# First attention scores ahead of the compressed values' copies, and an output slot's split behind the second head

## What is computed

```
kvc   = silu(blocks(kv) @ cmp_w1) @ cmp_w2            # compressed keys k_cmp and values v_cmp, 15 blocks
p_cmp = softmax(q @ k_cmp * scale - slope * dist)     # branch 1
p_slc = softmax(q @ k_slc * scale - slope * dist)     # branch 2, all 4 blocks of 64 are selected
p_win = softmax(q @ k_win * scale - slope * dist)     # branch 3, window 512 > 256 tokens
o     = g0 * p_cmp @ v_cmp + g1 * p_slc @ v_slc + g2 * p_win @ v_win
x     = x + o @ w_out
```

## Time and profile before

| what | value |
|---|---|
| runs | 1428.94 us median of 3 (1428.84 to 1434.26) |
| profiled execution | 1427.04 us, of it the span of the profile 1425.3 us |
| TensorE busy | 1387.1 us, 97% of the span |
| VectorE busy | 1182.6 us, 83% |
| ScalarE busy | 1020.8 us, 72% |
| chain that ended last, by engine | PE 91%, DVE 4%, issue 1%, ACT 1%, DMA 1% |
| mean granted clock of TensorE | 0.994 |
| moved from HBM | 429.40 MB, 302 GB/s over the span |

### The profile page before, as it was taken

One profiled execution on the slowest core, in us unless ns is written; L12 is line 12 of the kernel. 1 busy time (PEld: TensorE's weight loads), 2 busy tenths in 40 slices (PEclk: granted clock), 3 DMA queues, 4 the chain that ended last, 5 costly groups with the idle time before them and its releaser, 6 DMA issues.

```text
span 1425.3 us, 19022 instructions
## 1 busy us (share of the span) xinstructions
PE 1387.1 (97%) x6962; PEld 1139.1 (80%) x6962; DVE 1182.6 (83%) x1094; ACT 1020.8 (72%) x1070; POOL 41.1 (3%) x99
## 2 busy tenths in 40 slices
PE   7999999999999989999999999999999999999996
PEld 7987888888974578788888878888878888878884
DVE  6946655547768679899999999999999999999997
ACT  6546544435557757788887888887888888788884
POOL 7000000001000000000000000000000000000000
PEclk9999999999999989999999999999999999999999
DMA  8443555554630029899999999999999999999995
GB/s 325 168 172 118 207 178 182 175 205 148 237 119 1 21 113 351 322 391 421 408 398 402 397 394 406 404 409 401 392 400 395 414 412 394 388 415 384 421 421 206
DMA packets 59995, 431.68 MB, mean 303 GB/s; under 512 B 6656, under 2 KB 6656, under 8 KB 7808
## 3 DMA queue, kind: packets, MB, share of 16 engines
q1 hardware_dynamic: 59760, 429.95, 77.2%
q10 hardware_dynamic: 144, 0.52, 0.1%
HBM read 429.40 MB, written 1.05 MB: 302 GB/s over the span
## 4 chain that ended last, share of the span: by engine, by line
PE 91%; DVE 4%; issue 1%; ACT 1%; DMA 1%; DVEq 0%; POOL 0%; POOLq 0%; SPq 0%; ACTq 0%
PE bank L1509 19%; PE bank L1511 19%; PE bank L1510 19%; PE bank L1980 7%; PE bank L1981 6%; PE bank L2060 3%; PE bank L1999 3%; PE bank L2000 3%; DVE w_lo L1376 2%; PE bank L1857 2%; PE bank L1883 2%; PE bank L1951 1%; PE bank L1867 1%; PE bank L2047 1%; DMA raw<-in_moe 1%
## 5 line engine op out<-in xcount | busy, mean ns | idle before, releaser
L1376 DVE TENSOR_TENSOR w_lo<-raw,w_hi 128x2048 fp32r<-128x2048 f32 x331 | 747.0, 2287 | 38.7 <-ACT w_hi L759 36.0
L759 ACT ACTIVATE w_hi<-raw 128x2048 fp32r<-128x2048 f32 x331 | 630.2, 1919 | 127.5 <-PE bank L1511 57.8
L1509 PE MATMUL bank<-w_hi,ht_hi 128*128 128x512 f32 (+1 forms) x768 | 299.4, 390 | 0.9 <-DVE ht_lo L908 0.9
L1511 PE MATMUL bank<-w_hi,ht_lo 128*128 128x512 f32 (+1 forms) x768 | 296.3, 386 | 0.0
L1510 PE MATMUL bank<-w_lo,ht_hi 128*128 128x512 f32 (+1 forms) x768 | 295.8, 385 | 0.0
L876 DVE TENSOR_TENSOR w_lo<-raw,w_hi 128x2048 fp32r<-128x2048 f32 x73 | 166.6, 2289 | 109.9 <-ACT w_hi L444 109.7
L444 ACT ACTIVATE w_hi<-raw 128x2048 fp32r<-128x2048 f32 x74 | 141.5, 1919 | 95.0 <-PE bank L1511 92.9
L1980 PE MATMUL bank<-w_hi,ht_hi 128*128 128x512 f32 x448 | 177.4, 396 | 1.4 <-DVE w_lo L1376 1.4
L1981 PE MATMUL bank<-w_lo,ht_hi 128*128 128x512 f32 x448 | 174.7, 390 | 0.0
L1509 PEld LDWEIGHTS bank<-w_hi,ht_hi 128*128 128x128 f32 x768 | 144.4, 188 | 29.6 <-issue 1.4
L1511 PEld LDWEIGHTS bank<-w_hi,ht_lo 128*128 128x128 f32 x768 | 144.3, 188 | 29.5
(11 more groups left out here) (338 smaller groups left out, 1666.0 us busy)
## 6 DMA issues: line engine op xcount, KB each, us to landing
raw<-in_moe SPq DMA_DIRECT2D x336, 1024.0 KB, 7.6
raw<-in_wts SPq DMA_DIRECT2D x71, 1024.0 KB, 4.9
xs<-in_x SPq DMA_DIRECT2D x2, 512.0 KB, 4.1
out<-xn SPq DMA_DIRECT2D x4, 256.0 KB, 2.0
pk<-in_packed SPq DMA_DIRECT2D x1, 517.0 KB, 7.8
g1b<-in_norm_ffn ACTq DMA_DIRECT2D x1, 512.0 KB, 3.8
gfb<-in_norm_final SPq DMA_DIRECT2D x1, 512.0 KB, 8.4
```

Of the source, the lines that this page charges most:

```text
L759: a(w_hi[:, n % SPLIT, :], raw[:, n % RAW, :], ACT.Copy).then_inc(s_hi, 1)
L1376: v.tensor_tensor(w_lo[:, n % RAW, :], raw[:, n % RAW, :], w_hi[:, n % SPLIT, :].bitcast(F32), ALU.subtract).then_inc(s_lo, 1)
L1509: mm(out_, sh, mh, start=first, stop=False)
L1511: return mm(out_, sl, mh, start=False, stop=last)
```

## The change

The first scores' wait for all six copies of the compressed keys and values is taken out. The compressed scores wait for the two key copies (`s_kc >= 2`), and the transposes of turn 1, which write the bank that the values are copied from, wait for all six. The call `split_to(BO0 + 1)` moves on ACT from ahead of turn 0's exponentials into turn 1, behind turn 2's exponentials, and on DVE from ahead of turn 0's bias into turn 1, behind turn 3's bias. The work itself is the same.

```diff
@@ scalar: behind the six copies of kc and vbd
-        split_to(BO0 + 1)
@@ scalar: in the loop over n
             if n + 1 < 2 * HB:
                 head_exp(n + 1)
+            if n == 1:
+                split_to(BO0 + 1)
             if n in (2, 8):
                 cmp_exp(n // 8)
@@ tensor: behind the compression matmuls
         ins.then_inc(s_w2, 1)
-        pe.wait_ge(s_kc, 6)
@@ tensor: behind the first scores
         for n in range(3):
             head_scores(n)
+        pe.wait_ge(s_kc, 2)
         cmp_scores(0, range(HB // 2))
@@ tensor: in the loop over n
+            if n == 1:
+                pe.wait_ge(s_kc, 6)
             head_transpose(n)
```

## The result

The changed kernel took 1440.8 us (median of 20 runs, 1430.51 to 1444.06), the kernel before, run beside it, 1429.46 us (20 runs, 1426.19 to 1434.26). The ratio is 1.0074, with a 95% interval of 1.0063 to 1.0084. That is 11.3 us slower, where the prediction had 0.7 us and a range that ended at 1432.5 us. It was wrong.

A forecast was written before the change was run, and what follows sets the result against it. PE was taken to bound the kernel (91% of the last-ending chain). Wait removed -2.12, turn 3's transposes' wait +1.7, lost lead and late copy +1.1: +0.7 us, 1429.6 us; 8-in-10 range 1426.3 to 1432.5.

The forecast's parts named there:

- cover left behind it on ACT: Idle time remaining on ACT between its moved split and the copy of turn 0's transposes: 1.7 us, so the move is free.
- Parts 1 to 3: First scores: PE gains 2.12 us; ACT's split costs nothing; DVE's two splits take 4.4 us, making compressed sums 1.36 late.
- What is late next: PE waits 1.7 us ahead of turn 3's transposes, then for group 0's product, ending 0.65 to 0.7 us behind.
- Rival A: DVE's lateness dies out before reaching PE, so the whole gap is won: -2.1 us, 1426.8 us; chance 0.18.
- The rule cited beside it: Find gaps on the busiest engine and let what their semaphores depend on start or end sooner; by it, 1426.8 us.
- Rivals B and C: B: ACT and DVE set the pace behind the splits, +1.4 to +2.3, 0.14. C: first scores still held, +2.8, 0.03.
- rival D: A new 1.7 us gap on PE brings the granted clock down to 0.50 for about 2 us: +2 more; chance 0.02.

The follow-up runs named there:

- e5: The changed kernel plus 7 spare matmuls on PE ahead of turn 3's transposes, half filling the new gap: 1429.69 us, ratio 0.9996 to the kernel before.
- e3: The changed kernel plus 14 spare matmuls on PE ahead of turn 3's transposes, filling the new gap: 1429.96 us, ratio 1.0001 to the kernel before.
- e1: The kernel before with only PE's waits moved, the splits staying ahead of the heads: 1427.39 us, ratio 0.9977.
- e2: The changed kernel with the wait for all six copies back ahead of the first scores, so only the splits are moved: 1438.85 us, ratio 1.0063.
- e6: The kernel before with ACT's split moved ahead of the key and value copies, lengthening PE's old gap to 3.02 us: 1431.51 us, ratio 1.0002.
- e7: e1 plus spare matmuls while PE waits at the router, 22 ahead of the ranks and 11 behind them: 1425.94 us, ratio 0.9966 to the kernel before.
- e9: The changed kernel plus 20 spare matmuls on PE ahead of turn 6's transposes, its gap kept: 1439.14 us, ratio 1.0061 to the kernel before.

## Why the prediction was wrong, step by step

Its steps on the schedule held. With 1.70 us taken off the times of the changed kernel (0.08 off that of e5):

| step | forecast | measured |
|---|---|---|
| idle ahead of the first scores | 0 | 0 |
| DVE's first bias | 403.1 | 404.85 - 1.70 = 403.15 |
| ACT's split | 409.6 | 411.26 - 1.70 = 409.56 |
| cover left behind it on ACT | 1.7 | 1.72 (the bracket at 414.88) |
| DVE's two splits | 414.0, 4.4 long | 413.92, 4.48 |
| compressed bias | 418.4 | 418.32 |
| ACT's scaling, turns 2 and 3 | 420.0, 424.15 | 419.91, 424.04 |
| PE's wait ahead of turn 3's transposes | 1.7 | 1.66 |
| group 0's product (clock at 1.00, e5) | near 429.0 | 429.01 - 0.08 = 428.93 |
| lag of the output projection (clock at 1.00, e3 and e5) | +0.7 | +0.55 |

**Parts 1 to 3** and **What is late next** were right, in mechanism and in size; the sum was 0.15 us too high for the schedule. The two runs of the change that held the clock, 1430.51 and 1431.04 us, are 1.1 and 1.6 us above the median of before, where the forecast had 0.7. **Rival A** didn't come: the whole gap is won in e1 (2.19 us), without the second half of the change, and not in the change itself. The rule cited beside it from the Trainium skill, "Perfetto Trace Analysis", section "Optimization Strategy", is borne out by e1 and misleads for the change, in which the waits of 2.12 and 1.66 us are two different ones. **Rivals B and C** didn't come.

**The step that failed is the clock behind the new gap.** The sum priced the wait of turn 3's transposes at its length, +1.7, and put what the clock does behind it at nothing; only rival D had it, with a chance of 0.02 and a price of +2. It named the mechanism, a new gap of 1.7 us that takes the clock to 0.50. Measured, the half clock lasted 27 us and cost 11.4 us (+11.91 of the head stretch, against +0.55 with the gap filled). Two things were wrong in rival D.

- The ground for dismissing it: "the gap of 2.12 us that goes was longer and left the clock at 1.00." That compares gaps by length alone. Two gaps of 1.66 us at the new place took the clock in 18 of 20 and 7 of 7 runs, one of 3.02 at the old place in perhaps 1 of 10. And the trace of before has a counterexample: at 339 us waits of at most 1.45 us, with about 1 us of work between them, were followed by the half clock. A wait of a length is no measure by itself. What differs between the two places could also be read there. Ahead of the old gap stands a projection (PE and PEld both busy for 2.00 of 2.00 us in 396 to 398), and behind it 4 us of head and compressed scores and then a projection again. The new gap stands where the projection ends and nothing but heads follows, in which PEld was busy 3.46 of 7.00 us, some 64 us of it, up to the output projection at 489.77. Whether that difference is the reason isn't shown. But the evidence of one gap elsewhere was slight, and 0.02 far too sure.
- The price. "+2" took the half clock to last as long as the stretch of 2 us in the earlier trace rows. But in that stretch PE did nothing, and the question was how long the clock stays down once there is work. Even in the trace of before the answer was longer: at the router it was 0.81 in 519 to 520 and 0.51 on average in 520 to 530, with matmuls in 6 of these 10 us. Here it stayed down 27 us, of which 26.7 were busy, and the four groups above show what that costs.

The Trainium skill, "TensorE: Matmul & The Clock Gate", in its part on the HAM clock gate, was weighed and set aside as not borne out by the trace at this length. That an idle array loses half its clock is what happened in the change: 0.84 in 425 to 426, then 0.50. In e2 it fell only when PE had been at work again for 0.5 us.

The range was built from what the other cases cost, 1426.8 to 1431.7 us, and rival D at its real price, about +11, had no place in it. Had its chance been put where such slight evidence should have left it, at 0.2 or more, its price would have had to be worked out and the range would have had to reach 1440.

## What to carry to other kernels

Take out a wait on the bounding engine by itself, and leave the work that fills the other engines' idle time where it is: one half of this change was worth -2.2 us, the other turned it into +11.9. Price a new gap on TensorE by how long the clock could stay down behind it as well (3.4 to 27 us in the traces here), not by its own length alone and not by another gap that did no harm, and look for every stretch at half clock that the trace already has. Where a gap can't be avoided, a few spare matmuls on data that is there anyway can keep the clock (seven of 128x256 were enough here), and at the router they shortened a stretch at half clock.

## What the runs showed that had not been expected

- Continuous work doesn't bring the clock back at once: PE was busy for 26.70 of 27 us at 0.50, with PEld busy 14.11, in the heads; and in e6 for the last 5 us at 0.50 PE and PEld were both busy throughout, in a projection.
- The clock falls without a gap too. At the router it begins to fall in logits of 16 and 8 columns that follow each other: 0.81 in 519 to 520 us, with PE and PEld busy for the whole of it. In e7 it fell in spare matmuls of 128x256. Timeline and stretch, kernel before:

```profile
519.70 0.36 PE L1934 MATMUL bank<-ws_hi,ht_lo 128*128 128x8 f32 x1
```

```profile
519.00:520.00 1.00, 1.00 (x10) 1.00 (x9) 1.00 (x4) 0.47 (x2) 0.55 (x1) 0.81 1.04 442
```

- The same program can hold the clock or lose it: 2 of 20 runs of the change held it, and 2 of 8 of e9.

Four things stay open: what makes a run hold the clock; why it stays down 27.3 us in the change and 13.7 in e2, with the same matmuls behind the gap; why the new place loses it so much more often than the old one, since no run put the same gap into other work; and whether the moment at which a gap comes counts, which no run varied by itself.
